# Mixture-of-experts block: down products of pairs 0 to 13 in 64-column tiles, and their sums over all 128 rows

## The chip, the cores and the metric

The kernel runs on one core of a Trainium2 chip. The metric is the device time of one launch in microseconds. Its engines work side by side, each through its own queue of instructions: TensorE (PE, with its weight loads as PEld), VectorE (DVE), ScalarE (ACT), GpSimd (POOL) and SyncE (SP), which here issues the weight transfers. They wait for one another through semaphores.

## What is computed

Two transformer layers are followed by a third one with 32 experts, all float32, for 256 tokens of width 1024. Only the experts matter here. Each token picks two of them; in the reference, cut to that part:

```python
def run_block(args):
    toks, wts, e = args
    xb = hf[toks]
    y = (jax.nn.silu(xb @ w_gate[e]) * (xb @ w_up[e])) @ w_down[e]   # 1024 -> 512 -> 1024
    return y * wts[:, None].astype(y.dtype)

ys = lax.map(run_block, (slot_tok.reshape(n_blocks, MOE_BLOCK),
                         slot_w.reshape(n_blocks, MOE_BLOCK), block_expert))
out = jnp.zeros((N, D), h.dtype).at[slot_tok].add(ys.reshape(n_slots, D).astype(h.dtype))
```

## The kernel before

**Slots.** The experts are worked off in 16 pairs (`PAIRS`). Each expert has 32 slots (`SL`) for chosen tokens of the first half (tokens 0 to 127) and 32 for the second (`NT` = 2 halves), so a pair has 128 slots. Tokens are moved with products by 0/1 matrices: `pick` gathers token rows into slots, and `pickw`, which holds the token's weight for the expert in place of the 1, brings the results back. If an expert has more tokens than slots, further passes follow in a loop (`pair`); on these inputs one pass does.

**A pair's steps on PE**, for pair n, in the order in which `block.tensor` writes them: in `up(n)` the gate products into bank 0 (`expand`, L1648), then the sums of pair n - 2 (`sum_up`, L1659), then the up products into bank 1; then for pair n - 1 `rows_down` (L1694), `hidden_turned` (L1681, the transposes of pair n's hidden values), `picks_turned` (L1687, the transpose of the 128 x 128 picks of pair n - 1), and `next_rows` (L1603), the gathers for a later pair. The residual rows (L1666) are added once each between up and down of four pairs, after `RESIDUAL_AT` = 9, and a product into bank 3 (L1755) stands ahead of pair 13's down products.

**Shapes.** The slots stand in the order expert, half, place as columns of `xs` and of `hidT`. The gate and up products take 64 of these columns (an expert's) as stationary operand and stream 512 columns of its weights; the pair's two experts use the two column halves of the array. `down` takes 32 columns, those of one expert and one half, and puts the result at row `2 * SL * t + SL * e`, so that the rows of y stand in the order half, expert, place. A pair has four such products for each k of 4 and each half of the 1024 output columns. `sum_half` then multiplies, for each token half t, rows 64 t to 64 t + 63 of the turned picks and of `yE` into bank 4 + 2 t + half:

```python
r = 2 * SL * t
sums.append(mm(moe_bank[4 + 2 * t + half][:, :], weights[r:r + 2 * SL, :], yE[r:r + 2 * SL, 512 * half:512 * half + 512], ...
```

**VectorE's part.** In its loop for i it makes `hidden(i + 1)` (L3314), copies y of pair i from banks 2 and 3 to `yE` (`rows_back`, L3331), the turned hidden values (`hidden_back`, L3320) and the turned picks (`picks_back`, L3325), scales the gathered rows (`rows_in_two`, L3307), and writes the next pair's weighted picks (`pick_weights`, L3292) and picks (`pick_rows`, L3281).

**Weights.** A pair has six weight blocks of 2 MB: gate, up and down for two experts. SP issues them in a fixed order (`LOAD_ORDER`) into 11 slots (`NXS`). Ahead of each issue it waits until the slot's old content has been used (`chunk_used`): for gate, up and down blocks on `gate_full`, `up_full` and `y_full`, which PE raises at the end of these products. The last blocks are issued in parts (L703, L714).

Of the kernel before, what the change touches and what calls it, by code (L numbers as in the profile page):

```python
# [20 lines left out]
ALU = mybir.AluOpType  # L21
AX = mybir.AxisListType

P = 128
# [3 lines left out]
NT = SEQ // P  # L28
# [186 lines left out]
def program(nc, d, out):  # L215
# [15 lines left out]
    with ExitStack() as ctx:  # L231
# [176 lines left out]
        pick = bc[:, 0:256].rearrange("p (t j) -> p t j", t=NT)  # L408
        pickw_rows = bc[:, 256:384]
        pickw = pickw_rows.rearrange("p (t e j) -> p e t j", e=2, t=NT)  # L410
        pickT = bc[:, 384:512]
        hidE = bc[:, NBC2:NBC2 + DE]
        silE = mflat[:, 512:1024]
        hidT = mflat[:, 0:512].rearrange("p (k n) -> p k n", k=KE)
# [386 lines left out]
        def _(pe):  # L801
# [116 lines left out]
            for layer in range(DEPTH):  # L918
# [320 lines left out]
                def down(j, name, first, last):  # L1239

                    pairs = 2 if j < DOWN_CHUNKS - 1 else KF // 2 - 2 * j
                    return seven(T("dn"), name, hid_blocks(2 * j, pairs), lambda s_: hsum[:, j % 2, s_], down_blocks(ch + j, pairs),
                                 lambda s_: wsum[:, (FFN_CHUNKS + j) % 2, s_, 0:512 * pairs].rearrange("p (a n) -> p a n", a=pairs), first, last)
# [419 lines left out]
            def residual(i):  # L1663
# [2 lines left out]
                mm(moe_bank[4 + i][:, :], ident[:, :], xn[:, t, :].rearrange("p (k j) -> p j k", k=KD)[:, 64 * half:64 * half + 64, :],  # L1666
                   start=False, stop=True, skip_group_check=True)

            def sum_up(n, first, weights=pickT):

                for half in range(2):
                    pe.wait_ge(sem(f"y_ready{half}"), n + 1)
                pe.wait_ge(sem("pickT_ready"), n + 1)
                for half in range(2):
                    sum_half(half, first, weights)
# [8 lines left out]
            def picks_turned(n, o=0):  # L1684

                pe.wait_ge(sem("pickw_ready"), n + 1)
                nc.tensor.transpose(moe_bank[1][:, o:o + P], pickw_rows, ident[:, :]).then_inc(sem("pickT_full"), 1)  # L1687

            def down(n, w, half, k, rows=hidT, first_bank=2):

                for e in range(2):
                    for t in range(NT):
                        at, src = 2 * SL * t + SL * e, TILE_COLS * e + SL * t
                        ins = mm(moe_bank[first_bank + half][at:at + SL, :], rows[:, k, src:src + SL], w[e](2 * k + half),  # L1694
                                 start=(k == 0), stop=(k == KE - 1), skip_group_check=True)
                return ins
# [1 line left out]
            def down_weights(n):  # L1698
                return [landed(n, 4 + e) for e in range(2)]

            def rows_down(n):

                w = down_weights(n)
                if isinstance(n, int) and n == 0:
                    for k in range(KE):
                        for half in range(2):
                            ins = down(n, w, half, k)
                            if k == KE - 1:
                                ins.then_inc(sem("y_full"), 1)
                        if k == 1:  # L1710
                            ins.then_inc(sem("early_parts_read"), 1)
                    return
                for half in range(2):
                    for k in range(KE):
                        ins = down(n, w, half, k)
                    ins.then_inc(sem("y_full"), 1)

            def up(n):

                if 1 < n < PAIRS - 1:  # L1720
                    pe.wait_ge(sem("hidT_ready"), n)
                if n > 1 and n < PAIRS - 1:
                    pe.wait_ge(sem("pickT_ready"), n - 1)
                if n in (0, PAIRS - 1):
                    half_ready, all_ready = n * 2 + 1, n * 2 + 2
                else:
                    half_ready, all_ready = [4 + 4 * ((n - 1) // 2) + 2 * part for part in range(2)]
                inside = (lambda: gather_two(0, 1, 6, 0)) if n == 1 else None
                expand(n, 0, 0, half_ready, all_ready, inside).then_inc(sem("gate_full"), 1)
                if n == 0:  # L1730
                    chosen_counts()
                if n > 1:
                    sum_up(n - 2, n == 2)
                expand(n, 2, 1, half_ready, all_ready).then_inc(sem("up_full"), 1)

            def next_rows(n):
# [11 lines left out]
            for n_ in range(PAIRS - 2):  # L1748
                up(n_ + 1)
                if RESIDUAL_AT <= n_ < RESIDUAL_AT + 2 * NT:  # L1750
                    residual(n_ - RESIDUAL_AT)
                pe.wait_ge(sem("hidT_ready"), n_ + 1)
                pe.wait_ge(sem("xs_ready"), min(6 + 2 * n_, 2 * PAIRS) if n_ else 4)
                if n_ == PAIRS - 3:
                    mm(moe_bank[3][:, :], ident[:, :], xn[:, 0, 0:512], start=True, stop=True, skip_group_check=True)  # L1755
                rows_down(n_)
                if n_ == PAIRS - 3:
                    pe.wait_ge(sem("y_ready0"), n_ + 1)
                    hidden_turned(n_ + 1, 2)
                else:  # L1760
                    hidden_turned(n_ + 1)
                picks_turned(n_)
                next_rows(n_)
            up(PAIRS - 1)
            w_late, w_last = down_weights(PAIRS - 2), down_weights(PAIRS - 1)
# [374 lines left out]
        def _(v):  # L2140
# [1143 lines left out]
            def pick_weights(i, n, before):  # L3284
# [7 lines left out]
                        ins = TS(pickw[:, e, t, :], place, r_, g_, ALU.is_equal, ALU.mult)  # L3292
                ins.then_inc(sem("pickw_ready"), 1)

            def rows_in(n, xs=xsE[1]):

                for q in range(2):
                    v.wait_ge(sem("xs_full"), n * 2 + q + 1)
                    TT(xs[:, 4 * q:4 * q + 4, 0:SLOTS2], moe_bank[2 + q][:, 0:4 * SLOTS2].rearrange("p (k n) -> p k n", k=4),
                       g2c[:, 4 * q:4 * q + 4].unsqueeze(2).to_broadcast([P, 4, SLOTS2]), ALU.mult).then_inc(sem("xs_ready"), 1)  # L3300
# [21 lines left out]
            def picks_back(n, dst=pickT, o=0):  # L3322

                v.wait_ge(sem("pickT_full"), n + 1)
                nc.vector.tensor_copy(dst, moe_bank[1][:, o:o + P]).then_inc(sem("pickT_ready"), 1)  # L3325

            def rows_back(n, halves=range(2), first_bank=2):

                for half in halves:
                    v.wait_ge(sem("y_full"), n * 2 + half + 1)  # L3330
                    nc.vector.tensor_copy(yE[:, 512 * half:512 * half + 512], moe_bank[first_bank + half][:, :]).then_inc(sem(f"y_ready{half}"), 1)  # L3331
# [1 line left out]
            rows_in(0, xsE[0])  # L3333
            pick_rows(1, 4, 2)
            gates()
            pick_weights(0, 0, None)
            v.wait_ge(sem("count_full"), 1)
            nc.vector.reduce_max(cnt, bank(RANK_TILE[0])[:, 0:2 * NE], axis=AX.X).then_inc(sem("dve_step"), 1)
            step()
# [7 lines left out]
            for i in range(PAIRS - 2):  # L3347
                hidden(i + 1)
                rows_back(i)
                hidden_back(i + 1, bank=2 if i == PAIRS - 3 else 0)  # L3350
                picks_back(i)
                if i < PAIRS - 4:
                    rows_in_two(i // 2 + 1 if i % 2 == 0 else (i + 1) // 2, i % 2, 2)
                elif i == PAIRS - 4:
                    rows_in(PAIRS - 1)
                pick_weights(i + 1, i + 1, i + 1)
                if i % 2 and i + 4 < PAIRS:
                    pick_rows(i + 4, 4 if i + 5 < PAIRS else 2, 2 * i + 8)
            hidden(PAIRS - 1)
# [75 lines left out]
```

## Time and profile before

| | |
|---|---|
| median of 3 runs | 1597.59 us (1597.54 to 1599.92) |
| the profiled execution | 1597.35 us |
| its span, first to last instruction | 1595.5 us |
| PE busy | 1570.9 us, 98% |
| VectorE busy | 895.5 us, 56% |
| HBM read | 372.28 MB, 234 GB/s over the span |
| granted TensorE clock, mean | 0.998 |

The page and the views come from one profiled execution. A group of instructions is named by its line in the kernel, its engine and operation, the tensors it writes and reads, and its shape; for TensorE `128*64` means 128 rows by 64 columns of the array. One float32 product stands in the records as two matmuls. The chain of waits is followed back from the last instruction, at each step to whatever released it. The ends of matmuls are modelled, so two groups in a row can overlap a little. The experts fill the stretch from about 1156 us to 1588 us.

### The profile page before, as it was taken

The numbers are of one execution on the slowest core, as the hardware profiler recorded it, in microseconds if no ns is written. First come the engines' busy times: TensorE is split into PE (matmuls) and PEld (weight loads), VectorE is DVE, ScalarE is ACT, GpSimd is POOL, SyncE is SP. The second block draws the span as 40 slices with busy tenths as digits, with TensorE's granted clock in tenths as the row PEclk, the third lists the DMA queues.
The fourth block names the chain that finished last, engine by engine and source line by source line (L and its number), as shares of the span: only waits on it lengthen the run. The fifth ranks groups of instructions, "written<-read, shape, count | busy, mean of one in ns | idle before, by whom it ended". The sixth has DMA issues, their size and how long they took to land.

```text
span 1595.5 us, 20636 instructions
## 1 busy us (share of the span) xinstructions
PE 1570.9 (98%) x8777; PEld 998.7 (63%) x8777; DVE 895.5 (56%) x1549; ACT 192.5 (12%) x311; POOL 36.1 (2%) x60
## 2 busy tenths in 40 slices
PE   8999999999999999999999999999999999999997
PEld 4866499974458564999744876899533333333332
DVE  5896676765559876676646676795432223121122
ACT  1321000000114110000001331410000000000001
POOL 1001000000010010000000000000000000000000
PEclk9999999999999999999999999999999999999999
DMA  6532545563534336355536333446999999999997
GB/s 212 205 106 106 177 149 164 169 215 107 211 96 171 106 106 210 120 160 180 189 106 237 131 107 132 159 161 256 424 383 427 426 426 429 427 426 427 427 422 302
DMA packets 129781, 374.70 MB, mean 235 GB/s; under 512 B 17220, under 2 KB 65672, under 8 KB 116632
## 3 DMA queue, kind: packets, MB, share of 16 engines
q1 hardware_dynamic: 118864, 370.62, 61.1%
q10 hardware_dynamic: 10824, 2.72, 0.8%
q8 instruction: 72, 1.18, 0.3%
q14 instruction: 21, 0.17, 0.0%
HBM read 372.28 MB, written 1.05 MB: 234 GB/s over the span
## 4 chain that ended last, share of the span: by engine, by line
PE 88%; DMA 6%; SPq 3%; DVE 1%; issue 0%; ACT 0%; POOL 0%; POOLq 0%; DVEq 0%
PE bank L892 16%; PE bank L1204 16%; PE bank L823 10%; PE bank L1648 10%; PE bank L835 6%; PE bank L1694 5%; PE bank L1457 4%; DMA weights<-in_w_down 4%; SPq L703 3%; DMA arena<-in_w_up 3%; PE bank L1407 3%; PE bank L1329 2%; PE bank L1187 2%; PE bank L1490 2%; PE bank L1339 2%; PE bank L843 2%
## 5 line engine op out<-in xcount | busy, mean ns | idle before, releaser
L823 PE MATMUL bank<-weights,turned_rows 128*128 128x512 f32 x384 | 169.6, 598 | 0.4 <-DVE turned_rows L2167 0.4
L3314 DVE TENSOR_TENSOR bc<-mix,bank 128x512 f32<-128x512 f32 x16 | 17.2, 1077 | 212.6 <-PE bank L1648 212.6
L892 PE MATMUL bank<-arena 128*128 128x512 f32 x296 | 133.2, 592 | 0.0
L823 PEld LDWEIGHTS bank<-weights,turned_rows 128*128 128x128 f32 x384 | 72.7, 192 | 86.5 <-issue 85.9
L1204 PE MATMUL bank<-arena 128*128 128x128 f32 x960 | 110.5, 275 | 0.0
L1204 PEld LDWEIGHTS bank<-arena 128*128 128x128 f32 x960 | 108.8, 192 | 0.0
L892 PEld LDWEIGHTS bank<-arena 128*128 128x128 f32 x296 | 56.0, 190 | 69.9 <-issue 67.9
L835 PE MATMUL bank<-turned_rows,weights 128*128 128x256 f32 x448 | 98.6, 380 | 0.0
L1648 PE MATMUL bank<-arena,mix 128*64 128x512 f32 x304 | 92.3, 595 | 1.1 <-DMA arena<-in_w_up 0.6
L835 PEld LDWEIGHTS bank<-turned_rows,weights 128*128 128x128 f32 x448 | 84.6, 190 | 12.1 <-issue 0.7
L1694 PE MATMUL bank<-arena,mix 128*32 128x512 f32 x512 | 86.3, 594 | 2.5 <-DMA weights<-in_w_down 1.4
L1648 PE MATMUL bank<-arena,rows_late 128*64 128x512 f32 x224 | 78.2, 595 | 1.0 <-DMA weights<-in_w_up 0.7
L892 PE MATMUL bank<-weights,arena 128*128 128x512 f32 x172 | 78.8, 593 | 0.0
L1204 PE MATMUL bank<-turned_rows,weights 128*128 128x128 f32 x640 | 74.7, 275 | 0.0
L3331 DVE COPY bc<-bank 128x512 f32<-128x512 f32 x30 | 20.7, 692 | 95.5 <-PE bank L1694 95.5
L1204 PEld LDWEIGHTS bank<-turned_rows,weights 128*128 128x128 f32 x640 | 73.1, 192 | 0.0
L1831 ACT ACTIVATE arena<-bank 128x512 f32<-128x512 f32 (+1 forms) x68 | 38.2, 578 | 264.9 <-PE bank L823 141.2
L2240 DVE TENSOR_TENSOR arena<-weights 128x1024 f32<-128x1024 f32 (+1 forms) x22 | 25.9, 1176 | 77.3 <-PE bank L892 61.1
L767 POOL TENSOR_TENSOR st<-st,mhalf 128x1 f32<-128x1 f32 (+3 forms) x26 | 30.9, 1189 | 1549.8 <-DVE st L2272 517.6
L1694 PE MATMUL bank<-weights,mix 128*32 128x512 f32 x288 | 56.7, 593 | 2.1 <-DMA h<-in_w_down 0.8
L892 PEld LDWEIGHTS bank<-weights,arena 128*128 128x128 f32 x172 | 32.5, 190 | 40.2 <-issue 40.2
L1648 PE MATMUL bank<-weights,mix 128*64 128x512 f32 x144 | 56.6, 595 | 0.0
(542 smaller groups left out, 2490.4 us busy)
## 6 DMA issues: line engine op xcount, KB each, us to landing
weights<-in_w_in SPq DMA_DIRECT2D x28, 2048.0 KB, 7.9
arena<-in_w_gate SPq DMA_DIRECT2D x13, 2048.0 KB, 22.7
arena<-in_w_up SPq DMA_DIRECT2D x12, 2048.0 KB, 34.0
weights<-in_w_ffn_gate SPq DMA_DIRECT2D x22, 1024.0 KB, 5.4
weights<-in_w_ffn_up SPq DMA_DIRECT2D x22, 1024.0 KB, 8.1
weights<-in_w_ffn_down SPq DMA_DIRECT2D x10, 2048.0 KB, 7.8
arena<-in_w_down SPq DMA_DIRECT2D x10, 2048.0 KB, 29.7
weights<-in_w_out SPq DMA_DIRECT2D x8, 2048.0 KB, 8.3
```

The source lines that it names most:

```text
L703: sp.dma_start(expert_slot[at][:, width * part:width * part + width], wsrc[c6 + e][2 * n + e][:, width * part:width * part + width]).then_ ...
L823: ins = mm(b[:, :], xT[:, k, t0 + P * t:t0 + P * t + P], w[:, k, :], start=(k == 0), stop=(k == KD - 1))
L835: ins = mm(b[:, o:o + nt], w[:, k, P * m:P * m + P], xT[:, k, n0:n0 + nt], start=(k == 0), stop=(k == KD - 1))
L843: ins = nc.tensor.transpose(b[:, q * j:q * j + q], src[0:q, at:at + P], ident[0:q, 0:q])
L892: ins = mm(b[:, :], lhs[:, j, :], rhs[:, j, :], start=(first and j == 0), stop=(last and j == pairs - 1))
L1187: ins = mm(b[:, o:o + P], w[:, k, P * f:P * f + P], xT[:, k, NM + P * t:NM + P * t + P], start=(k == 0), stop=(k == KD - 1))
L1204: ins = mm(b[:, o + P * q:o + P * q + P], lhs[:, q, k, :], rhs[:, k, :], start=(k == 0), stop=(k == 3))
L1407: ins = mm(b[:, 256 * m:256 * m + 256], slot(uc, KD, 512)[:, k, P * (2 * (u % 2) + m):P * (2 * (u % 2) + m) + P], xT[:, k, NM:NTOK], start ...
L1457: ins = mm(b[:, o + P * m:o + P * m + P], lhs[:, m, k, :], rhs[:, k, :], start=(k == 0), stop=(k == 3))
L1648: ins = mm(moe_bank[bank][TILE_COLS * e:TILE_COLS * e + TILE_COLS, :], xs[:, k, o + TILE_COLS * e:o + TILE_COLS * e + TILE_COLS], w[e](k), ...
L1694: ins = mm(moe_bank[first_bank + half][at:at + SL, :], rows[:, k, src:src + SL], w[e](2 * k + half), start=(k == 0), stop=(k == KE - 1), s ...
L1831: act.activation(dst, src, func, **kw).then_inc(psum_free(tile), 1)
```

## The change

Pairs 0 to 13 get a second form of the down products and the sums; pairs 14 and 15 and the loop for further passes keep the first. `wide_down` takes all 64 columns of an expert, so there are two products instead of four for each k and half, and the rows of y stand in the order expert, half, place. `wide_pick_weights` writes one 128-column block of weighted picks for each token half, in which the other half's columns stay zero (they are zeroed once). `wide_picks_turned` turns both blocks, `wide_picks_back` copies 256 columns into what was the router's weights, and `wide_sum_up` multiplies for each token half all 128 rows of its turned block with all 128 rows of `yE`: four products of 128 rows instead of four of 64.

```diff
--- before.py
+++ after.py
@@ -408,7 +408,10 @@
         pick = bc[:, 0:256].rearrange("p (t j) -> p t j", t=NT)
         pickw_rows = bc[:, 256:384]
         pickw = pickw_rows.rearrange("p (t e j) -> p e t j", e=2, t=NT)
-        pickT = bc[:, 384:512]
+        wide_pickw_rows = [bc[:, 256 + P * t:256 + P * t + P] for t in range(NT)]
+        wide_pickw = [v.rearrange("p (e t j) -> p e t j", e=2, t=NT) for v in wide_pickw_rows]
+        wide_pickT = wrt.rearrange("p k n -> p (k n)")[:, 0:NT * P]
+        pickT = wide_pickT[:, 0:P]
         hidE = bc[:, NBC2:NBC2 + DE]
         silE = mflat[:, 512:1024]
         hidT = mflat[:, 0:512].rearrange("p (k n) -> p k n", k=KE)
@@ -1666,6 +1669,16 @@
                 mm(moe_bank[4 + i][:, :], ident[:, :], xn[:, t, :].rearrange("p (k j) -> p j k", k=KD)[:, 64 * half:64 * half + 64, :],
                    start=False, stop=True, skip_group_check=True)
 
+            def wide_sum_up(n):
+
+                for half in range(2):
+                    pe.wait_ge(sem(f"y_ready{half}"), n + 1)
+                pe.wait_ge(sem("pickT_ready"), n + 1)
+                for half in range(2):
+                    for t in range(NT):
+                        mm(moe_bank[4 + 2 * t + half][:, :], wide_pickT[:, P * t:P * t + P], yE[:, 512 * half:512 * half + 512],
+                           start=(n == 0), stop=True, skip_group_check=True)
+
             def sum_up(n, first, weights=pickT):
 
                 for half in range(2):
@@ -1685,6 +1698,21 @@
 
                 pe.wait_ge(sem("pickw_ready"), n + 1)
                 nc.tensor.transpose(moe_bank[1][:, o:o + P], pickw_rows, ident[:, :]).then_inc(sem("pickT_full"), 1)
+
+            def wide_picks_turned(n):
+
+                pe.wait_ge(sem("pickw_ready"), n + 1)
+                for t in range(NT):
+                    ins = nc.tensor.transpose(moe_bank[1][:, P * t:P * t + P], wide_pickw_rows[t], ident[:, :])
+                ins.then_inc(sem("pickT_full"), 1)
+
+            def wide_down(w, half, k):
+
+                for e in range(2):
+                    at = TILE_COLS * e
+                    ins = mm(moe_bank[2 + half][at:at + TILE_COLS, :], hidT[:, k, at:at + TILE_COLS], w[e](2 * k + half),
+                             start=(k == 0), stop=(k == KE - 1), skip_group_check=True)
+                return ins
 
             def down(n, w, half, k, rows=hidT, first_bank=2):
 
@@ -1698,18 +1726,26 @@
             def down_weights(n):
                 return [landed(n, 4 + e) for e in range(2)]
 
-            def rows_down(n):
+            def wide_rows_down(n):
 
                 w = down_weights(n)
-                if isinstance(n, int) and n == 0:
+                if n == 0:
                     for k in range(KE):
                         for half in range(2):
-                            ins = down(n, w, half, k)
+                            ins = wide_down(w, half, k)
                             if k == KE - 1:
                                 ins.then_inc(sem("y_full"), 1)
                         if k == 1:
                             ins.then_inc(sem("early_parts_read"), 1)
                     return
+                for half in range(2):
+                    for k in range(KE):
+                        ins = wide_down(w, half, k)
+                    ins.then_inc(sem("y_full"), 1)
+
+            def rows_down(n):
+
+                w = down_weights(n)
                 for half in range(2):
                     for k in range(KE):
                         ins = down(n, w, half, k)
@@ -1730,7 +1766,7 @@
                 if n == 0:
                     chosen_counts()
                 if n > 1:
-                    sum_up(n - 2, n == 2)
+                    wide_sum_up(n - 2)
                 expand(n, 2, 1, half_ready, all_ready).then_inc(sem("up_full"), 1)
 
             def next_rows(n):
@@ -1753,13 +1789,13 @@
                 pe.wait_ge(sem("xs_ready"), min(6 + 2 * n_, 2 * PAIRS) if n_ else 4)
                 if n_ == PAIRS - 3:
                     mm(moe_bank[3][:, :], ident[:, :], xn[:, 0, 0:512], start=True, stop=True, skip_group_check=True)
-                rows_down(n_)
+                wide_rows_down(n_)
                 if n_ == PAIRS - 3:
                     pe.wait_ge(sem("y_ready0"), n_ + 1)
                     hidden_turned(n_ + 1, 2)
                 else:
                     hidden_turned(n_ + 1)
-                picks_turned(n_)
+                wide_picks_turned(n_)
                 next_rows(n_)
             up(PAIRS - 1)
             w_late, w_last = down_weights(PAIRS - 2), down_weights(PAIRS - 1)
@@ -3292,6 +3328,17 @@
                         ins = TS(pickw[:, e, t, :], place, r_, g_, ALU.is_equal, ALU.mult)
                 ins.then_inc(sem("pickw_ready"), 1)
 
+            def wide_pick_weights(n):
+
+                if n:
+                    v.wait_ge(sem("pickT_full"), n)
+                for t in range(NT):
+                    for e in range(2):
+                        r_ = rank[:, t, n * 2 + e:n * 2 + e + 1]
+                        g_ = gate[:, t, n * 2 + e:n * 2 + e + 1]
+                        ins = TS(wide_pickw[t][:, e, t, :], place, r_, g_, ALU.is_equal, ALU.mult)
+                ins.then_inc(sem("pickw_ready"), 1)
+
             def rows_in(n, xs=xsE[1]):
 
                 for q in range(2):
@@ -3324,6 +3371,11 @@
                 v.wait_ge(sem("pickT_full"), n + 1)
                 nc.vector.tensor_copy(dst, moe_bank[1][:, o:o + P]).then_inc(sem("pickT_ready"), 1)
 
+            def wide_picks_back(n):
+
+                v.wait_ge(sem("pickT_full"), n + 1)
+                nc.vector.tensor_copy(wide_pickT, moe_bank[1][:, 0:NT * P]).then_inc(sem("pickT_ready"), 1)
+
             def rows_back(n, halves=range(2), first_bank=2):
 
                 for half in halves:
@@ -3333,7 +3385,9 @@
             rows_in(0, xsE[0])
             pick_rows(1, 4, 2)
             gates()
-            pick_weights(0, 0, None)
+            nc.vector.memset(bc[:, 256:256 + NT * P], 0.0).then_inc(sem("dve_step"), 1)
+            step()
+            wide_pick_weights(0)
             v.wait_ge(sem("count_full"), 1)
             nc.vector.reduce_max(cnt, bank(RANK_TILE[0])[:, 0:2 * NE], axis=AX.X).then_inc(sem("dve_step"), 1)
             step()
@@ -3348,12 +3402,15 @@
                 hidden(i + 1)
                 rows_back(i)
                 hidden_back(i + 1, bank=2 if i == PAIRS - 3 else 0)
-                picks_back(i)
+                wide_picks_back(i)
                 if i < PAIRS - 4:
                     rows_in_two(i // 2 + 1 if i % 2 == 0 else (i + 1) // 2, i % 2, 2)
                 elif i == PAIRS - 4:
                     rows_in(PAIRS - 1)
-                pick_weights(i + 1, i + 1, i + 1)
+                if i < PAIRS - 3:
+                    wide_pick_weights(i + 1)
+                else:
+                    pick_weights(i + 1, i + 1, i + 1)
                 if i % 2 and i + 4 < PAIRS:
                     pick_rows(i + 4, 4 if i + 5 < PAIRS else 2, 2 * i + 8)
             hidden(PAIRS - 1)
```

## Rows read from the trace of the kernel before

**Rows 1.** Page: busy us (share), DMA tenths in 40 slices, a lone transfer's time to landing.
```profile
PE 1570.9 (98%) x8777; PEld 998.7 (63%) x8777; DVE 895.5 (56%) x1549; ACT 192.5 (12%) x311; POOL 36.1 (2%) x60
...
DMA  6532545563534336355536333446999999999997
...
weights<-in_w_in SPq DMA_DIRECT2D x28, 2048.0 KB, 7.9
```

**Rows 2.** Chain of waits, one pair of the PE-paced part: start us, us, what.
```profile
1379.03 2.02 PE bank L1603 x16
1381.05 7.02 PE bank L1648 x32
1388.07 1.92 PE bank L1659 x8
...
1397.01 7.05 PE bank L1694 x64
```

**Rows 3.** The same chain: the first and the last weight transfer in it.
```profile
1414.00 40.82 DMA weights<-in_w_down
...
1560.66 15.82 DMA weights<-in_w_down
```

**Rows 4.** Busy time by stretch: length, then busy us of PE, PEld, DVE, ACT, POOL.
```profile
1378.90:1404.78 25.88, 25.67 (x157) 9.47 (x157) 7.12 (x20) 0.60 (x1) 0.00 (x0) 1.00 1.01 428
...
1462.90:1492.30 29.40, 27.72 (x159) 10.61 (x159) 5.42 (x12) 0.60 (x1) 0.00 (x0) 1.00 1.01 426
```

**Rows 5.** Who waited for whom (us, times, longest), PE: 1196 to 1404, then from 1404.
```profile
PE bank L1603 <- DVE bc L3331: 1.7, 8, 0.2
...
PE bank L1694 <- DMA weights<-in_w_down: 1.9, 3, 0.8
...
PE bank L1648 <- DMA turned_rows<-in_w_gate: 0.2, 1, 0.2
```

**Rows 6.** Timeline: start us, us, engine line op, operands [idle before <-releaser].
```profile
1396.94 7.07 PE L1694 MATMUL bank<-arena,mix 128*32 128x512 f32 x64
...
1397.39 0.13 PEld L1694 LDWEIGHTS bank<-arena,mix 128*32 128x32 f32 x4 [0.30 <-issue]
...
1403.94 0.65 PE L1681 MATMUL bank<-ident,bc 128*128 128x128 f32 x4
...
1404.43 0.27 PE L1687 MATMUL bank<-ident,bc 128*128 128x128 f32 x1
...
1404.91 2.02 PE L1603 MATMUL bank<-bc,xn 128*128 128x128 f32 x16 [0.21 <-DVE bc L3331]
1405.28 0.28 DVE L3325 COPY bc<-bank 128x128 f32<-128x128 f32 x1
1406.08 0.69 DVE L3307 TENSOR_TENSOR rows_late<-bank,g2c 128x512 f32<-128x512 f32 x1 [0.52 <-PE bank L1603]
...
1414.42 0.19 PEld L1659 LDWEIGHTS bank<-bc 64*128 64x128 f32 x2 [0.24 <-issue]
```

**Rows 7.** Chain of waits: gate and up products of pair 1 in one run.
```profile
1177.77 12.17 PE bank L1648 x56
```

**Rows 8.** Full-array products of 512 columns: chain of waits, and line L1490's forms.
```profile
1115.75 16.31 PE bank L1490 x38
...
1142.59 3.53 PE bank L1490 x8
...
L1490 PEld LDWEIGHTS bank<-weights,mix x64: 190/190/192, 1115.5 to 1145.1; 128*128 128x128 f32 x64
```

**Rows 9.** Line L1666, moving operand strided: ns min/median/max.
```profile
L1666 PE MATMUL bank<-xn,ident x8: 1040/1076/1113, 1422.8 to 1511.9; 128*128 128x512 f32 x8
```

**Rows 10.** Timeline of VectorE behind the first picks' weights.
```profile
1164.02 0.23 DVE L3338 TENSOR_REDUCE s<-bank 128x1 f32<-128x64 f32 x1 [1.31 <-PE bank L1576]
```

**Rows 11.** DMA issues at 1215.9 and at 1536.1 us: KB, us to landing.
```profile
arena<-in_w_gate SPq DMA_DIRECT2D x1, 2048.0 KB, 11.2
...
arena<-in_w_down SPq DMA_DIRECT2D x1, 512.0 KB, 26.9
```

## The prediction, made before the changed kernel was run

> **What bounds the kernel now.** I read the page first. TensorE (PE) is busy 98% of the span, and from the 29th of the 40 slices on, which is where the experts run, the DMA engines are busy nine tenths or more too [rows 1]. So two things are nearly full together, and the question is which of them releases the end, and how far behind the other is.
>
> The chain of waits answers for each stretch. Up to about 1404 us it is PE's own work, in a cycle of 25.88 us for each pair of experts (from the gathers at 1379.03 to those at 1404.91): gathers 2.02, the gate products of a pair 7.02, the sums of an older pair (L1659) 1.92, the up products 7.02, the down products (L1694) 7.05, then 0.85 until VectorE has copied the second half of y [rows 2, 6]. After 1414 the chain goes by weight transfers, the first of 40.82 us from issue to landing, and by SP's issuing, up to one that lands at 1576.48 [rows 3]. The same cycle is 29.4 us long there instead of 25.88, and the DMA engines move 426 to 428 GB/s in both [rows 4]. PE had started with a store of loaded weights, drew on it by 3.5 us a pair, and had used it up at pair 9.
>
> How much does PE wait for weights once the store is empty? The list of who waited for whom puts 1.9 + 1.3 + 1.0 + 0.8 + 0.8 + 0.7 + 0.2 = 6.7 us in ten waits on DMAs between 1404 and the end (seven lines, of which the first and the last stand in the rows). Between 1196 and 1404 its only line is 1.7 us on VectorE [rows 5]. Where PE doesn't wait, a product's modelled end reaches about 0.07 us past the next start (1396.94 + 7.07 against 1403.94) [rows 6]; each of the ten waits is hidden by so much. With that the waits are 6.7 + 10 x 0.07 = 7.4, and I take 7.5 (bounds 6.7 and 7.7). This is all the slack that PE has; the chain's long DMA pieces show which resource paces the stretch, not how much PE could be slowed.
>
> **The change part by part.** *Down products, pairs 0 to 13.* Four products of 32 columns at a time become two of 64 columns. A float32 product has two records. Before, 64 records take 7.05 us; the gate and up products are already of the new form, 64 columns for each of two experts, and 32 records of them take 7.02 [rows 2]. Both are sixteen steps: the old down products load their weights four at a time in steps of 0.13 + 0.30 = 0.43 us [rows 6], and so (7.02 against 7.05) must the gate products, two at a time. What is streamed (512 columns per step) doesn't change, so the smaller count of instructions buys nothing: 0.
>
> *Change of tile shape.* Before, PE changes its tile shape between up and down; after, both have 64 columns. Gate and up of pair 1 already follow each other without a change of shape: 24 + 32 records in 12.17 us, where 32 alone cost 7.02 [rows 7]. At 0.429 us a step [rows 8] the joined 28 steps are 12.01 and have 0.16 of overhead, as much as 16 steps alone (7.02 - 6.86): where two runs join, one overhead of 0.16 is saved (bounds 0 and 0.22). That holds for pairs 0 to 8; pairs 9 to 13 have a full-array product in between (L1666, L1755). 9 x 0.16 = -1.4 us.
>
> *Sums.* Before, the four products of a pair use 64 rows each, and the two token halves run side by side in the two row halves: 8 records in 1.92 us, four steps of 0.43 [rows 2]. After, each has 128 rows, nothing can run beside it, and the 8 records are eight steps. Full-array products of 512 columns show their price elsewhere: 38 records in 16.31 us, or 0.429 each, and 8 in 3.53 [rows 8]. 8 x 0.429 + the 0.20 of overhead that the present sums have = 3.63; so +1.71 a pair, with 1.61 (from 3.53) as the lower bound. The upper bound is a row with a strided moving operand, 1.076 us a record [rows 9]; the new sums read yE contiguously, so I stay with the contiguous rows. They run inside the up steps of pairs 2 to 15, fourteen times, on the path of PE: 14 x 1.71 = +23.9 us.
>
> A row and a rule differ here. In the row the 190 ns weight load of each full-array product is hidden, since 38 of them follow each other at the streaming rate [rows 8]. The Trainium skill, "TensorE: Matmul & The Clock Gate", Part 3, says that a weight load overlaps a running product only when their row groups differ, which they don't in full-array products. By the row the sum stays as above; by that rule it would be the second rival below.
>
> *One more transpose of picks.* One record, 0.12 us by the step of the four before it. It stands between the down products and the gathers, where PE now waits 0.21 us for VectorE's copy of y [rows 6], so 0.1 of cover is left. Pair 13 has no gathers behind it: +0.1 once. Without that cover it would be 14 x 0.12 = 1.7.
>
> *VectorE.* The copy of the turned picks doubles from 128 columns (0.28 us) to 256, 0.14 more, a third of the way to the 0.69 of a 512-column copy. It stands ahead of the g2 multiplications, before which VectorE waits 0.52 us for the gathers [rows 6]: hidden, 0.4 left. The picks' four multiplications keep their size. The memset of 256 columns with its wait comes once, ahead of work that waits 1.31 us for the counts [rows 10]; no row shows a memset of 256 columns, but one as long as the 0.69 of a 512-column copy would be covered. The new waits on pickT are for copies made a whole pair earlier: 0. The bounds of all this with the transposes are 0 and +1.7.
>
> *Does the slower PE starve the DMA queue?* A slot is freed when PE has used it, so SP issues later. A 2 MB transfer alone takes 7.9 us to land [rows 1]. At 1215.9, the first issue behind the new sum, landing takes 11.2 [rows 11], so 3.3 us of work stand ahead of it; the issue moves by 1.6, and 1.7 are left. Behind that the queue still grows each pair by 29.4 less PE's cycle, which is 27.4 then instead of 25.88, so by 2.0. At 1414 landing takes 40.8 [rows 3], against a shift of 14. The tail has the other low point: at 1536 landing takes 26.9, so 19 stand ahead [rows 11] against a shift of 14 to 15. So the DMA engines never run dry, and the last weights land when they do now, at about 1576 to 1584.
>
> **The sum.** Ahead of the first wait for weights PE is late by 9 x 1.71 - 9 x 0.16 = 14.0 us. From there to pair 12 its cycle would be 25.88 + 2.0 (the residual product: 27.7 of busy time a cycle instead of 25.67 [rows 4]) + 1.71 = 29.6, as long as the 29.4 of the stream, so it stays some 14 us behind the weights and no longer waits for any. All 7.5 us of waiting go, and PE is the bound from beginning to end. The profiled execution is 1597.35 us (1595.5 of span), 0.24 under the median of 1597.59, which I neglect:
>
> 1597.35 + 23.9 - 1.4 + 0.1 - 7.5 = 1612.45, so 1612.5 us.
>
> **Rivals.**
> *Not slower: the down products give it back.* Place: the down step of each of 14 pairs. If the four 32-column products hindered each other, two of 64 columns would be shorter. The point from which it decides: PE's net addition has to be under 7.5 / 14 = 0.54 a pair, so down has to fall by 1.71 - 0.54 = 1.2, from 7.05 to 5.9 or less. Then DMA paces the end, 1597.5 us. For it: half the instructions. Against it: the equal 7.02 and 7.05 of both forms [rows 2]. Chance 0.06.
> *Weight loads come into the open.* The wide sums would pay 8 x 0.19 = 1.5 us more a pair: 14 x 1.5 = 21, so 1633.5 us. Against it stand the 38 records of [rows 8]; what speaks for it is only that those stand in a long run, and the sums will be eight between products of another shape. Chance 0.04.
> *The queue runs dry.* A hole in the transfers moves all landings behind it. Since PE runs 14 us behind them, only a hole beyond 14 us costs; one of 20 us gives 1612.5 + 6 = 1618.5. It decides only if the 1.7 us at 1215.9 and the growth behind it are read wrongly. Chance 0.05.
> *The change doesn't do what it says:* the wide products of the two token halves go to different banks and overlap after all. Then the addition is 0.2 or less a pair and the time is 1597.5. All 128 rows are taken, so I give it 0.02.
>
> **How the numbers follow.** Forecast 0.80, the rivals 0.06, 0.04, 0.05 and 0.02, and 0.03 for something not thought of. For the range: with 1.61 a pair and the full 0.22 saved in all 14, 1597.35 + 22.5 - 3.1 - 7.7 = 1609; with no saving, an uncovered transpose and copy, and 2 us of waits that stay, 1597.35 + 23.9 + 1.7 - 5.5 = 1617.5. I add what the third rival reaches and a little below: 1607 to 1619. 0.2% is 3.2 us, about what a measurement of this kernel can tell from no change. Slower takes the forecast, the second and third rival and half of the unknown: 0.91. Within 0.2% takes most of the first and fourth: 0.06. Faster: 0.03, if down falls well under 5.9 and the stream itself gains.
>
> **What the profile of after would show.** The chain has L1659's successor at 3.6 us and the down products at 6.9 to 7.05, in cycles of 27.4 us before pair 9 and 29.4 to 29.6 with the residual products. PE's waits for DMAs between 1404 and the end are gone, and the chain has next to no DMA in it. The DMA share falls in the last slices, and the time from issue to landing near 1414 falls from 41 to about 27 us. The last weights still land near 1576 to 1584, 12 us or more before PE uses them. The prediction is wrong if down's 16 steps are shorter than 0.43, if a wide sum isn't near 3.6, or if waits for weights remain.

## The result, and the profile after

The changed kernel takes 1612.23 us (median of 4 runs, 1612.05 to 1612.52), the kernel before in the same comparison 1597.92 us. The ratio is 1.0084, with a 95% interval of 1.0071 to 1.0098: slower by 14.3 us. The forecast was 1612.5, with a range of 1607 to 1619. The profiled execution took 1612.2 us, of which 1610.2 are span, so it is 14.7 us of span longer than the one before.

Two rows of the page of after. The DMA engines stay at nine tenths up to the last slice but one, as before, but in the last slice they are busy 3 tenths where they were 7 [rows 1]: their work is done earlier, seen from the end.

```profile
PE 1594.3 (99%) x8343; PEld 1011.0 (63%) x8343; DVE 897.4 (56%) x1550; ACT 192.5 (12%) x311; POOL 36.0 (2%) x60
...
DMA  6532545562633325454536234556999999999993
```

The chain of waits of after, one pair, as [rows 2] (start us, us, what). L1606 are the gathers, L1651 gate and up, L1679 the wide sums, L1713 the wide down products, L1694 and L1706 the transposes of hidden values and of picks:

```profile
1389.92 2.02 PE bank L1606 x16
1391.94 7.02 PE bank L1651 x32
1398.96 3.63 PE bank L1679 x8
1402.59 7.02 PE bank L1651 x32
1409.61 6.87 PE bank L1713 x32
1416.47 0.59 PE bank L1694 x4
1417.06 0.22 PE bank L1706 x2
1417.28 0.08 issue
1417.36 2.02 PE bank L1606 x16
```

Against [rows 2] the sums went from 1.92 to 3.63 and the down products from 7.05 to 6.87. The 7.05 ends at a modelled end, the 6.87 where the transposes start, so the two are not quite alike; from the start of the down products to that of the gathers it was 7.90 us (1397.01 to 1404.91) and is 7.75 (1409.61 to 1417.36). The cycle from gathers to gathers (1389.92 to 1417.36) is 27.44 us instead of 25.88. VectorE's copy of y, which closed the cycle before, has left the chain: PE goes from the down products through two lots of transposes to the gathers.

From pair 9 on a residual product stands between up and down, and at the end the chain still is on PE, up to the last sums:

```profile
1430.03 7.02 PE bank L1651 x32
1437.05 1.91 PE bank L1669 x2
1438.95 7.02 PE bank L1713 x32
...
1600.51 2.01 PE bank L1662 x8
```

The cycles with a residual product are 29.5 us long (1417.36 to 1446.86). There is no weight transfer in this chain, where [rows 3] had one of 40.82 us and one that landed at 1576.48. The list of who waited for whom, for PE from 1170 us to the end, has one line left, and none of the DMA lines of [rows 5]:

```profile
PE bank L1651 <- DVE mix L3354: 0.4, 1, 0.4
```

Busy time of two stretches as in [rows 4] (length, then busy us of PE, PEld, DVE, ACT, POOL, clock, DMA share, GB/s): in a window as long as the stream's cycle PE is now busy without a break, while the DMA engines go on at the same rate:

```profile
1378.90:1404.78 25.88, 25.80 (x122) 10.14 (x120) 7.24 (x19) 0.60 (x1) 0.00 (x0) 1.00 1.01 428
1462.90:1492.30 29.40, 29.32 (x130) 10.87 (x128) 5.57 (x11) 0.60 (x1) 0.00 (x0) 1.00 1.01 427
```

The timeline around the gathers, the answer to [rows 6] (start us, us, what), and the memset with what follows it, the answer to [rows 10]:

```profile
1416.90 0.38 PE L1706 MATMUL bank<-ident,bc 128*128 128x128 f32 x2
...
1417.36 2.02 PE L1606 MATMUL bank<-bc,xn 128*128 128x128 f32 x16
1417.73 0.41 DVE L3377 COPY wrt<-bank 128x256 f32<-128x256 f32 x1
1418.53 0.69 DVE L3354 TENSOR_TENSOR rows_late<-bank,g2c 128x512 f32<-128x512 f32 x1 [0.39 <-PE bank L1606]
```

```profile
1162.02 0.27 DVE L3388 MEMSET bc<- 128x256 f32 x1
...
1164.16 0.22 DVE L3392 TENSOR_REDUCE s<-bank 128x1 f32<-128x64 f32 x1 [0.92 <-PE bank L1579]
```

The second transpose ends just ahead of the gathers, which show no idle time any more, where there were 0.21 us. The copy of the picks is 0.41 us long instead of 0.28, and VectorE waits 0.39 us behind it instead of 0.52. The memset took 0.27 us, and VectorE still waited 0.92 us behind it.

Last, three issues of weight transfers with their time to landing, at 1217.6, 1426.4 and 1546.2 us; they answer to [rows 11] and the first of [rows 3]:

```profile
arena<-in_w_gate SPq DMA_DIRECT2D x1, 2048.0 KB, 9.6
```

```profile
weights<-in_w_down SPq DMA_DIRECT2D x1, 2048.0 KB, 27.6
```

```profile
arena<-in_w_down SPq DMA_DIRECT2D x1, 512.0 KB, 16.1
```

The first was 11.2 us and is 9.6, so 1.7 us of work stood ahead of it if 7.9 is a lone transfer's time [rows 1]. The second was 40.8 and is 27.6. The third was 26.9 and is 16.1. None of them comes down to a lone transfer.

### The profile page after: what moved, and what is told of

Same layout as the page of the kernel before. It is cut to its first block, busy times and chain, and to the rows that moved or that the text cites. A ratio compares the mean times of both kernels' runs of the same rounds, so it can differ in the third digit from the quotient of the medians.

```text
span 1610.2 us, 19769 instructions
## 1 busy us (share of the span) xinstructions
PE 1594.3 (99%) x8343; PEld 1011.0 (63%) x8343; DVE 897.4 (56%) x1550; ACT 192.5 (12%) x311; POOL 36.0 (2%) x60
## 4 chain that ended last, share of the span: by engine, by line
PE 97%; DVE 1%; DMA 1%; issue 0%; SPq 0%; POOL 0%; ACT 0%; POOLq 0%; DVEq 0%
PE bank L895 16%; PE bank L1207 16%; PE bank L1651 14%; PE bank L826 10%; PE bank L838 6%; PE bank L1713 6%; PE bank L1460 4%; PE bank L1679 3%; PE bank L1410 3%; PE bank L1332 2%; PE bank L1190 2%; PE bank L1606 2%; PE bank L1493 2%; PE bank L1342 2%; PE bank L846 2%; PE bank L1364 1%
## 5 line engine op out<-in xcount | busy, mean ns | idle before, releaser
L1651 PE MATMUL bank<-arena,mix 128*64 128x512 f32 x304 | 92.3, 596 | 0.4 <-DVE mix L3354 0.4
L1651 PE MATMUL bank<-arena,rows_late 128*64 128x512 f32 x224 | 78.1, 596 | 0.0
L1713 PE MATMUL bank<-arena,mix 128*64 128x512 f32 x208 | 71.3, 593 | 0.0
L2148 ACT ACTIVATE mix<-bank 128x512 f32<-128x512 f32 x16 | 9.6, 597 | 403.0 <-PE bank L1651 403.0
L1651 PE MATMUL bank<-weights,mix 128*64 128x512 f32 x144 | 56.6, 595 | 0.0
```

Source lines behind the costliest of these rows:

```text
L1651: ins = mm(moe_bank[bank][TILE_COLS * e:TILE_COLS * e + TILE_COLS, :], xs[:, k, o + TILE_COLS * e:o + TILE_COLS * e + TILE_COLS], w[e](k), ...
L1713: ins = mm(moe_bank[2 + half][at:at + TILE_COLS, :], hidT[:, k, at:at + TILE_COLS], w[e](2 * k + half), start=(k == 0), stop=(k == KE - 1) ...
```

## The experiments

The theory to be tested: in the kernel before the weight stream sets the end, though the chain of waits shows PE's own work up to about pair 9, and PE has a slack of some 7.5 us. What the change adds on PE is free up to that slack and counts in full beyond it. The rivals are that each addition on PE counts in full or by a share, that the stream alone or PE alone sets the time, and that the wide down products have a price or a gain of their own. Each kernel is compared with the kernel before, on the same chip. The diffs are cut at `...`; those of e5 and e6 are against the kernel before, the others against the changed one.

### One half of the change at a time

*e1: wide down products, sums of before.*

```diff
-                    wide_sum_up(n - 2)
+                    sum_up(n - 2, n == 2)
...
-                wide_picks_turned(n_)
+                picks_turned(n_)
...
-            wide_pick_weights(0)
+            pick_weights(0, 0, None)
...
```

> The changed kernel with its wide down products, but the sums and picks of before: four sum products of 64 rows. Rows of y then stand by expert and the picks by token half, so the sums of pairs 0 to 13 add wrong rows; only the time is of use. Theory (the weight stream ends the kernel, PE has about 7.5 us of slack): the 9 x 0.17 = 1.5 us that PE gains become waits for weights, 1597.5 to 1597.9 us, level with before. Rival (PE's work is the bound by itself): 1596.4. Rival (two products of 64 columns are cheaper than four of 32): down products under 6.5 us a pair in the trace; the theory says 6.87, and 7.02 for pairs 9 to 13.

Measured: 1596.56 us against 1598.31, ratio 0.9991 (0.9981 to 1.0). Its chain has the sums of before beside the wide down products:

```profile
1262.76 1.92 PE bank L1662 x8
1264.68 7.02 PE bank L1651 x32
1271.69 6.89 PE bank L1713 x32
```

So the down products cost 6.89 in this form (6.87 in after), and the first rival of the prediction, down at 5.9 or less, is out. The time is on the low side of what the slack allows; this is taken up again below.

*e2: sums over 128 rows, down products of before.*

```diff
-        wide_pickw = [v.rearrange("p (e t j) -> p e t j", e=2, t=NT) for v in wide_pickw_rows]
+        wide_pickw = [v.rearrange("p (t e j) -> p e t j", e=2, t=NT) for v in wide_pickw_rows]
...
-                wide_rows_down(n_)
+                rows_down(n_)
```

> The other half alone: down products in 32-column tiles as before, sums over all 128 rows as after, the zeroed picks laid out for rows of y in the order half, expert, place. Theory: the whole cost is in the sums, 3.63 us a pair against 1.92, and the nine saved changes of tile shape are gone: 1612.2 + 1.6 = 1613.8 us. Rival (the wide down products cost or give something of their own): away from 1613.8 by 14 times that, so 1.4 us for each 0.1 us a pair.

Measured: 1614.07 us, ratio 1.0093 (1.0076 to 1.011), against 1613.8 expected. Its chain:

```profile
1178.31 12.17 PE bank L1651 x56
...
1262.62 3.63 PE bank L1679 x8
1266.25 7.02 PE bank L1651 x32
1273.27 7.00 PE bank L1722 x64
...
1438.86 1.91 PE bank L1669 x2
```

The down products of 32 columns take 7.00 here, the wide sums 3.63 as in after. All of the cost is in the sums. What the wide down products give back is read by setting this chain beside that of after, which has the first and the last of these pieces at

```profile
1177.92 12.17 PE bank L1651 x56
...
1437.05 1.91 PE bank L1669 x2
```

Against after, e2 is 0.39 us later ahead of the down products of pair 0 and 1.81 later ahead of those of pair 9. So the nine pairs 0 to 8 gave 1.42, or 0.16 a pair. From there to the end the distance stays at 1.81 to 1.83, so pairs 9 to 13 gave nothing. The 0.39 us was there before any down product ran and isn't theirs. The medians say the same: 15.76 us above before in e2 and 14.31 in after, so 1.45 between them, though from two comparisons.

### How much PE work is free

*e3 and e4: the wide form for pairs 0 to 4, and for pairs 0 to 8.* The diff of e3; e4 has 9 in place of 5.

```diff
-                    wide_sum_up(n - 2)
+                    if n - 2 < 5:
+                        wide_sum_up(n - 2)
+                    else:
+                        sum_up(n - 2, False)
...
-                wide_rows_down(n_)
+                if n_ < 5:
+                    wide_rows_down(n_)
+                else:
+                    rows_down(n_)
...
-                if i < PAIRS - 3:
+                if i + 1 < 5:
                     wide_pick_weights(i + 1)
```

> The wide form for pairs 0 to 4 only. Theory (additions on PE are free up to its slack of 7.5 us): 5 x 1.54 = 7.7 us more on PE, so 0.2 us more in time, 1598.0 us, and the waits for weights nearly gone. Rival (each wide pair costs its share of the 14.5): + 5.2, 1603.0 us. Rival (no slack, all 1.54 a pair count): + 7.7, 1605.5 us.

> The wide form for pairs 0 to 8. Theory: 9 x 1.54 = 13.9 us on PE less 7.5 of slack, + 6.4, 1604.2 us. Rival (a share for each pair): + 9.3, 1607.2 us. Rival (no slack): 1611.7 us.

Measured: e3 1599.02 us against 1598.31, ratio 1.0003 (0.9994 to 1.0013), so + 0.7 with an interval of - 1.0 to + 2.1; a share for each pair (+ 5.2, a ratio of 1.0033) and the full count (+ 7.7) are both outside it. e4 1604.33 us, ratio 1.0035 (1.0023 to 1.0048), so + 6.0 where 6.4 was expected; a share (+ 9.3, 1.0058) and the full count are outside again. The first five wide pairs cost nothing that can be measured, the next four 5.3 us (1604.33 - 1599.02), and the last five 8.3 (14.3 above before, less 6.0). In e3 PE's waits from 1170 us on have no DMA among them any more, so its five pairs have about used up the slack:

```profile
PE bank L1606 <- DVE bc L3392: 1.5, 7, 0.2
PE bank L1651 <- DVE mix L3363: 0.4, 1, 0.4
PE bank L1592 <- DVE bc L3392: 0.2, 1, 0.2
```

### Which resource sets the end

*e5: the kernel before without the sums of pairs 1 to 13.*

```diff
-                    sum_up(n - 2, n == 2)
+                    if n == 2:
+                        sum_up(n - 2, True)
+                    else:
+                        for half in range(2):
+                            pe.wait_ge(sem(f"y_ready{half}"), n - 1)
+                        pe.wait_ge(sem("pickT_ready"), n - 1)
```

> The kernel before without the sums of pairs 1 to 13 (pair 0's stay, and the waits stay; the output lacks those experts' shares). PE has 13 x 1.92 = 25 us less to do. Theory (the weight stream is full from the start of the experts on and sets the end): 1597 to 1598 us, the 25 us turn up as waits for weights, 32 us in all. Rival (PE paces the experts until pair 9, and what it saves there counts): 1573 to 1590 us.

Measured: 1598.15 us against 1598.43, ratio 1.0 (0.999 to 1.0009). The work that was left out came back as waits for weights, of which these are the longest of eight lines (us in total, times, longest us):

```profile
PE bank L1648 <- DMA arena<-in_w_up: 10.7, 4, 3.0
PE bank L1694 <- DMA arena<-in_w_down: 5.7, 4, 2.7
PE bank L1648 <- DMA weights<-in_w_up: 3.9, 3, 1.7
PE bank L1648 <- DMA extra_slot<-in_w_up: 2.6, 1, 2.6
```

The eight lines make 27.4 us, where 32 were expected. Most of the rest is that PE itself was slower behind three waits of 2.6, 2.6 and 3.0 us, which ended at 1356.3, 1415.4 and 1446.1 us. Busy time in 10 us about each of them (columns as above), where the kernel before, whose longest wait is 1.0 us, has a clock of 1.00:

```profile
1355.00:1365.00 10.00, 8.66 (x32) 3.17 (x32) 0.00 (x0) 0.00 (x0) 0.00 (x0) 0.83 1.01 431
...
1412.00:1422.00 10.00, 7.43 (x28) 2.38 (x26) 0.00 (x0) 0.60 (x1) 0.00 (x0) 0.83 1.00 424
...
1443.00:1453.00 10.00, 6.96 (x28) 2.71 (x28) 0.00 (x0) 0.60 (x1) 0.00 (x0) 0.83 1.00 428
```

A mean of 0.83 is about a third of the 10 us at the lower of the two levels, 1.2 GHz. Three such stretches are 10 us in which PE ran at half speed, so its work took up to 5 us longer, by estimate; 4.6 were missing.

*e6 and e7: less weight traffic, in the kernel before and in the changed one.*

```diff
-                    expert_load(i % NXS, c6, n)
+                    if (n, c6) in [(7, 0), (7, 1), (8, 0), (8, 1)]:
+                        sp.dma_start(expert_slot[i % NXS][:, 0:64], wsrc[c6][2 * n + c6 % 2][:, 0:64]).then_inc(...)
+                    else:
+                        expert_load(i % NXS, c6, n)
```

> The kernel before with four weight transfers (gate weights of pairs 7 and 8) cut from 2 MB to a 64th, so that stale weights are used there: 4 x 4.9 = 19.6 us less for the DMA engines, PE's work unchanged. Theory: the weights come ahead, PE's 7.5 us of waits go and no more, 1590.2 us. Rival (the stream alone sets the end): 1578 us. Rival (PE has no slack worth the name): 1597.

> The changed kernel with the same four transfers cut. Theory: PE is the bound from end to end, nothing changes, 1612.2 us; against e6 that is + 22.0, which is PE's whole added work (14 x 1.71 - 9 x 0.18 + 0.1 = 22.4) without the slack. Rival (the stream still holds part of the time): 1605 to 1610 us.

Measured: e6 1590.14 us against 1598.43, ratio 0.995 (0.9933 to 0.9966), so - 8.3. e7 1612.38 us, ratio 1.0091 (1.0074 to 1.0108), against 1612.23 for the changed kernel with all its transfers. Of 19.6 us of transfers taken away the kernel before keeps 8.3 and the changed one nothing. PE's waits in e6 have no DMA left:

```profile
PE bank L1606 <- DVE bc L3334: 2.5, 12, 0.2
PE bank L1651 <- DVE mix L3310: 0.4, 1, 0.4
PE bank L1592 <- DVE bc L3334: 0.2, 1, 0.2
```

The two results together measure both terms of the prediction apart from each other: the slack is 8.3 us by the medians (1598.43 - 1590.14; 7.6 by the profiled executions, 1597.35 - 1589.76), and the work that the change adds on PE, with the stream out of the way, is 22.2 us (1612.38 - 1590.14), of which 14 remain.

### Whether the wide down products help the stream

e1 had come out 1.75 us below before. Two kernels look at that.

*e9: e1 again, more executions.* The kernel is that of e1.

> The kernel of e1 once more, in more rounds: wide down products, sums of before. e1 came out 1.75 us below before where the slack theory allowed 0 to 0.4, and its profiled execution had a stretch at half clock. Slack theory alone: level with before, within 0.5 us. Rival (a second effect: with two 64-column products in place of four of 32, PE reads each weight block once instead of twice, and the stream runs 1 us faster over the experts; from the 41st to the last landing it took 366.0 us in e1 and 365.7 in after, against 366.9 in before): 1.0 to 1.8 us below before.

*e8: wide down products, and no sums for pairs 1 to 13.*

```diff
-                    sum_up(n - 2, n == 2)
+                    if n == 2:
+                        sum_up(n - 2, True)
+                    else:
+                        ...
...
```

> As e5, the sums of pairs 1 to 13 left out, but with the wide down products. PE has 26 us less to do than before and only the stream can set the end. Slack theory alone: as e5, level with before, and the last weights land 367 us behind the 41st. Rival (the stream runs faster beside wide down products): 1.0 to 1.8 us below before, and 365.7 to 366.0 us.

Measured: e9 1596.89 us, ratio 0.9993 (0.9984 to 1.0002), and e8 1597.06, ratio 0.9997 (0.9988 to 1.0006), both against 1598.22. The medians are 1.3 and 1.2 us below before, in the direction and of the size of the rival, but both intervals hold 1. Yet 10 of the 11 executions of either kernel lie below the median of before, and e1's was 1.75 below on another chip, so a gain of about 1 us is likely. The landing times don't show where it comes from: from the 41st weight landing to the last it is 366.3 us in e9 and 365.6 in e8, and in kernels with down products of before 366.9 (before), 366.8 (e5) and 367.5 (e2). But e4, with wide down products in nine of its pairs, has 366.8 as well, where a gain pair by pair would have given less. One trace each is thin. It stays open whether the stream gains. That e8, with 25 us less of PE work than e9, is no faster than e9 agrees with e5: there is nothing to be had on PE alone.

e1's own profiled execution, at 1601.47 us, was above its median, and a row of it shows why, beside the same row of e9, which is the same kernel. Busy time from 1155 us (columns as above), e1 and then e9:

```profile
1155.00:1165.00 10.00, 10.00 (x42) 6.25 (x43) 6.05 (x26) 1.50 (x2) 0.00 (x0) 0.63 0.84 339
```
```profile
1155.00:1165.00 10.00, 10.00 (x54) 4.92 (x55) 6.92 (x32) 2.10 (x3) 0.00 (x0) 1.00 1.00 415
```

In e1 the granted clock was 0.63 from 1155 to 1165 us, a mixture of the two levels (2.4 and 1.2 GHz), and the DMA engines moved 339 GB/s in place of 415. The first refills wait for PE, and these are the issues in e1 and in e9:

```profile
1162.88 7.90 SPq L613 DMA_DIRECT2D arena<-in_w_up  x5
```
```profile
1158.50 7.92 SPq L613 DMA_DIRECT2D arena<-in_w_up  x5
```

They are 4.4 us apart, of which 0.5 were there ahead of the stretch. At 1536 to 1540 us the issues are still 3.8 us apart and the spans differ by 4.7: the delay stays to the end in a kernel that the stream paces. Why the clock fell in the one execution and not in the other isn't shown. e8's trace has less of it: 0.89 from 1140 to 1155 us and 0.99 from 1155 on, with the first refill at 1159.0. Its longest line of waits is of the size of e5's:

```profile
PE bank L1651 <- DMA arena<-in_w_up: 9.6, 4, 2.6
```

## Why the prediction was right

*What bounds.* Right, and the step on which all depends: the long DMA pieces in the chain [rows 3] showed the pacing resource, but the 7.5 us of waits [rows 5] showed the slack. Who had read only the chain would have called the change hidden; who had read only PE's 98% would have forecast 1597.35 + 22.6, 1620. e5 and e6 show both sides: 25 us less of PE work brought nothing, and 19.6 us less of transfers brought 8.3. That holds for the part ahead of 1404 us too, where the chain has only PE: about half of the sums that e5 leaves out stand there, and what PE saves there it waits for later.

*Sums.* 1.71 us a pair forecast, 3.63 - 1.92 = 1.71 measured, fourteen times. The contiguous full-array rows [rows 8] were the right neighbours, and the strided row the wrong one. Beside them the rule of the Trainium skill ("TensorE: Matmul & The Clock Gate", Part 3), that a weight load overlaps a product only when row groups differ, doesn't hold here: 3.63 us for eight records leaves no room for eight loads of 0.19. The same part of the Trainium skill also lets a load go ahead when it targets the background weight buffer; that would fit, but no run here shows which buffer is used. The second rival falls with it.

*Down products and the change of shape.* Forecast 0, and 0.16 a pair for nine pairs, 1.4 us. Right on both: against e2, which differs in the form of the down products alone, after gains 1.42 us over pairs 0 to 8 and nothing behind. The 7.05 and 6.87 of the two chains would make it 0.18 a pair, but they end differently, as said above.

*The second transpose.* Forecast as covered by the 0.21 us wait for VectorE, and 0.1 once at pair 13. From the start of the down products to that of the gathers the kernel before takes 7.90 us with one transpose (1397.01 to 1404.91), and e2, with the same down products and two transposes, 7.00 + 0.59 + 0.22 + 0.10 = 7.91. So it costs 0.01 us a pair: covered. In the working, the 0.69 us taken for a copy of 512 columns stands in [rows 6] for a multiplication; the copy of 256 columns measured 0.41, where 0.28 + 0.14 was forecast.

*The waits.* Forecast - 7.5, and this is the term that was off, by little. PE's work grew by 23.9 for the sums, less 1.4 for the change of shape, and 0.2 for the transposes (0.1 in all where they are covered, 0.1 at pair 13): 22.7 us, where e6 and e7 say 22.2. The profiled executions differ by 14.85, so 7.8 us of waits went; the medians differ by 14.31, so 8.4, and e6 says 8.3 by its medians and 7.6 by its profile. The slack was therefore taken 0.1 to 0.9 us too small. The forecast of 1612.5 still came out within 0.3 us, partly by luck: it forecast 15.1 us more and 14.3 were measured, but it started from a profiled execution of 1597.35 where the median of the comparison is 1597.92. The range had allowed for such errors.

*The queue.* The 1.7 us said to be left at the first issue behind the new sum were 1.7. The time to landing near 1414 was to fall to about 27 us, and is 27.6. From 1190 to 1550 us the DMA engines of after move as much as before (427 GB/s in both from 1200 to 1300), so the queue didn't run empty, and e7 shows that even with four transfers taken out nothing changes: the third rival is out. The last rival, that the wide sums overlap, is out by their 3.63 us. The last weights were to land near 1576 to 1584 us, as before; they land at 1583.0 in after and 1584.2 in before.

## What to carry to other kernels

When two resources are nearly full, the chain of waits names the one that paces the end, but what the other can still take is in the list of its waits: work added there was free up to about their sum and counted in full beyond it. That is shown for work ahead of the waits (e3, e4) and spread over them; no run put it behind the last wait, where there is nothing left to take it up. To join two products of 64 rows into one of 128 doesn't make them faster if they ran side by side in the two halves of the array's rows; count the steps in which the moving operand passes, not the instructions. Halving the instructions of the down products gave 0.16 us of 7, all of it by a saved change of tile shape, and the added steps of the sums cost ten times that.

## What the runs showed of the hardware that was not expected

Four executions of the changed kernel lie within 0.5 us of each other (1612.05 to 1612.52), those of kernels that the stream paces spread by several: 1595.93 to 1601.47 in ten of e1, 1597.47 to 1601.47 in ten of e3. One of e1's was traced, and there a stretch at a granted clock of 0.63 in front of the first refills had slowed the stream, which a later gain on PE can't make good. The others weren't traced, but each execution's mean clock is on record. The two slow ones of e1 (1600.37 and 1601.47) have 0.996 against 0.998 or 0.999 in its other eight, and so has the 1601.47 of e3; but 1600.07 and 1600.24 of e3 have 0.999 and 0.998, so the clock explains part of the spread and not all.

The same clock fell behind waits. In e5, PE did nothing for 2.6, 2.6 and 3.0 us, and each time about 3.4 us of the following work ran at half speed, by the rows of 0.83. It cost no time there: e5 is level with the kernel before, since the stream paces it and PE had time to spare.
